# Dividing a prompt's attention probabilities on ACT in place of DVE

## The reference

```
h = rmsnorm(x);  [u | q | k | v | forget | gates] = h @ w_in        # width 4616
s = q k^T / 8 + c_q - c_k, masked (k_pos <= q_pos)
p = softmax(s);  att = p @ v                                        # fox_block
x = x + (sig(g0) * (pool @ w_up_pool) + sig(g1) * (att @ w_up_att)) @ w_out
x = x + hier_moe(rmsnorm(x))     # top-1 of 4 groups, top-2 of its 8 experts, 32 experts in all
y = rmsnorm_final(x)
```

## Time and profile before

| | |
|---|---|
| time, median of 3 runs | 720.68 us (717.95, 720.68, 722.97) |
| span of the profiled execution, first to last instruction | 716.0 us |
| its own time outside the span | not among the timed runs; the median is 4.7 us above the span, the fastest run 1.95 us |
| busy, share of span | PE 83%, PE weight load 51%, DVE 31%, ACT 12%, POOL 7% |
| instructions | 13798; DVE 549, ACT 232 |
| HBM traffic | 269 MB in all, mean 376 GB/s |
| instructions of the touched step | 4 reciprocals, 16 multiplications on DVE |

### The profile page before, as it was taken

How to read it: one execution, slowest core, us unless ns; L and a number is a source line. 1 busy time by engine, 2 the same in 40 slices (tenths; PEclk the granted TensorE clock), 3 DMA queues, 4 the chain that set the end, 5 groups by cost and what they waited for, 6 DMA issues and landing times.

```text
span 716.0 us, 13798 instructions
## 1 busy us (share of the span) xinstructions
PE 597.4 (83%) x6181; PEld 367.5 (51%) x6181; DVE 222.2 (31%) x549; ACT 88.5 (12%) x232; POOL 51.3 (7%) x57
## 2 busy tenths in 40 slices
PE   8999999999999999999677678675877767786683
PEld 7778777775573555555343344343443334443341
DVE  4259996972140362322111111111111111111113
ACT  2312232311101330000000000000000000000003
POOL 4136430112000000000000000000000000000000
PEclk9999999999999999999898878898788988899887
DMA  9985989987999399999999999999999999999981
GB/s 303 303 334 208 326 181 426 376 350 315 411 424 415 126 376 407 422 423 427 424 424 424 423 427 428 421 424 424 427 424 422 426 426 425 424 422 427 420 350 73
DMA packets 41379, 269.15 MB, mean 376 GB/s; under 512 B 9845, under 2 KB 10673, under 8 KB 22880
## 3 DMA queue, kind: packets, MB, share of 16 engines
q1 hardware_dynamic: 28960, 229.34, 79.2%
q0 software_dynamic: 3072, 35.19, 12.0%
q10 hardware_dynamic: 9287, 3.73, 2.1%
HBM read 266.01 MB, written 2.46 MB: 375 GB/s over the span
## 4 chain that ended last, share of the span: by engine, by line
DMA 49%; PE 38%; DVE 6%; issue 3%; ACT 2%; ACTq 1%; POOL 0%; SPq 0%; DVEq 0%; POOLq 0%
DMA ring<-w_up 43%; PE bank L1371 11%; PE bank L1613 4%; PE bank L1630 4%; PE bank L1476 3%; DMA ring<-w_in 3%; PE bank L1544 2%; DVE ring L1025 2%; PE bank L1387 2%; DMA ring<-cache_k,ridx 2%; PE bank L1355 2%; PE bank L1567 2%; PE bank L1402 1%; PE bank L1462 1%; DMA x<-x_prompt 1%
## 5 line engine op out<-in xcount | busy, mean ns | idle before, releaser
L1371 PE MATMUL bank<-ring,front 128*32 128x256 f32 x1856 | 160.9, 482 | 89.2 <-DMA ring<-w_up 78.1
L1371 PEld LDWEIGHTS bank<-ring,front 128*32 128x32 f32 x1856 | 86.1, 138 | 147.2 <-issue 123.4
L1233 DVE COPY front<-bank 128x256 f32<-128x256 f32 x32 | 13.6, 425 | 235.1 <-PE bank L1371 235.1
L1567 PE MATMUL bank<-hT,ring 128*128 128x264 f32 x256 | 59.8, 389 | 1.5 <-DMA ring<-w_in 1.1
L1387 PE MATMUL bank<-ring,front 128*32 128x256 f32 x928 | 55.4, 379 | 0.0
L848 ACT ACTIVATE front<-bank 128x128 f32<-128x128 f32 x32 | 8.9, 278 | 372.9 <-PE bank L1379 372.9
L1567 PEld LDWEIGHTS bank<-hT,ring 128*128 128x128 f32 x256 | 47.7, 190 | 11.2 <-issue 2.1
L1355 PE MATMUL bank<-front 128*32 128x256 f32 (+1 forms) x768 | 52.3, 385 | 0.3 <-DVE front L1136 0.3
L1476 PE MATMUL bank<-hT,ring 128*128 128x264 f32 x192 | 44.6, 389 | 0.0
L1243 DVE COPY front<-bank 128x256 f32<-128x256 f32 x32 | 13.6, 425 | 86.7 <-PE bank L1387 86.7
L1387 PEld LDWEIGHTS bank<-ring,front 128*32 128x32 f32 x928 | 30.0, 110 | 20.1 <-issue 0.5
(11 more groups left out here) (322 smaller groups left out, 565.7 us busy)
## 6 DMA issues: line engine op xcount, KB each, us to landing
ring<-w_gate SPq DMA_DIRECT2D x28, 2048.0 KB, 41.9
ring<-w_up SPq DMA_DIRECT2D x28, 2048.0 KB, 38.7
ring<-w_down SPq DMA_DIRECT2D x28, 2048.0 KB, 41.3
ring<-w_in SPq DMA_DIRECT2D x8, 2048.0 KB, 21.5
x<-w_gate SPq DMA_DIRECT2D x3, 2048.0 KB, 42.4
x<-w_up SPq DMA_DIRECT2D x3, 2048.0 KB, 38.0
x<-w_down SPq DMA_DIRECT2D x3, 2048.0 KB, 41.9
ring<-w_out SPq DMA_DIRECT2D x2, 2048.0 KB, 16.5
```

Of the source, the lines that this page charges most:

```text
L1371: last = m.matmul(bank[GATEUP][32 * g:32 * g + 32, 0:256], xgT[:, k % 2, k // 2], w[:, k, 256 * (g % 2):256 * (g % 2) + 256], start=k == 0 ...
L1567: last = m.matmul(out[:, 0:TOK], w[:, k, cols], hT[:, k, 0:TOK], start=k == 0, stop=k == DK - 1)
```

## The change

ACT gets a step `hnorm`. It waits for a new semaphore that DVE counts after the reciprocal, and does the four multiplications as copies with a scale from a column of `hinv`. DVE keeps the reciprocal alone and no longer waits for it. PE's wait for `s_probs` stays, with ACT counting it. The list of steps isn't changed.

```
+        s_hinv = sem("prompt_sums_inverted")
@@ ACT's stream
+                elif step == "hnorm":
+                    act.wait_ge(s_hinv, a + 1)
+                    for f in range(2):
+                        pr = probs[:, f]
+                        s.activation(pr[:, 0:P], pr[:, 0:P], ACT.Copy, scale=hinv[:, f, 0:1])
+                        s.activation(pr[:, P:3 * P], pr[:, P:3 * P], ACT.Copy, scale=hinv[:, f, 1:2]).then_inc(s_probs, 1)
                 elif step == "pT":
@@ DVE's stream
                     elif step == "hnorm":
                         dve.wait_ge(s_exp, 4 * a + 4)
-                        link(v.reciprocal(hinv, hsum))
-                        for f in range(2):
-                            pr = probs[:, f]
-                            v.tensor_scalar(pr[:, 0:P], pr[:, 0:P], hinv[:, f, 0:1], None, ALU.mult)
-                            v.tensor_scalar(pr[:, P:3 * P], pr[:, P:3 * P], hinv[:, f, 1:2], None, ALU.mult).then_inc(s_probs, 1)
+                        v.reciprocal(hinv, hsum).then_inc(s_hinv, 1)
```

## The result

The changed kernel takes 724.43 us (723.06 to 725.83, four runs) against 719.54 us for the kernel before in the same comparison: 4.9 us more, a ratio of 1.0070 with a 95% interval of 1.0041 to 1.0099. It is slower, clear of scatter, and within 1%. The profiled execution has a span of 722.8 us against 716.0.

The account below looks back on a forecast made before the run. PE's progress to SP's load at 248.81 us, then fixed loading, was taken as the bound. Stall 4.7 plus clock 1.9 less 0.86 gave 5.7 us over 720.7: 726.4 us, range 722 to 730.

Parts of the forecast that it names:

- the sum of 5.7 us: Whole kernel: 4.7 us of stall plus 1.9 of slower clock less 0.86 of saved wait, against the profiled execution.
- Pair 0 behind ACT's issues: At pair 0, ACT's copies wait behind its load issues; PE idles 4.1 us and `gate` 2 starts 4.7 us late.
- The copies: On ACT, four scaled copies per pair take 1.49 us, at least 1.1; the first f is ready after 0.79.
- The clock: After PE's pause at 94.3 us, a lower clock lengthens `gate` 2 by 1.9 us, bounds 0 and 2.9.
- The gain of 0.86 us: PE's wait for `m1` at 154.51 us goes away, which is all the change can gain.
- Pair 1 to 3 hidden: At pairs 1 to 3, the copies fit beside PE's gates and DVE has 4 us to spare: no further stall.
- the two waits of 1.7 and 2 us: DVE loses about 1.7 us at pair 2 and waits about 2 us at pair 3, behind late exponentials.
- The end moves one for one: Any delay of PE before SP's load at 248.81 us delays the kernel's end by the same amount.
- the one without a stall: Rival at pair 0: ACT's issues don't block the copies, only the 0.86 us is gained: 719.8 us, chance 0.12.
- the stall without the clock: Rival at pair 0: PE pauses but its clock stays up or drops under a microsecond: 724.5 us, chance 0.13.
- the table load: Rival at ACT's copies: table loads before and after, 8 x 1.28 us, mostly hidden: 728 us, chance 0.03.
- A second wait: Rival: PE also waits for a late `m1` or pair 3's copies, or a longer low clock: 728.5 to 731 us, chance 0.2.

Follow-up runs that it names:

- e1: The changed kernel, with ACT issuing the eight router loads after pair 0's division instead of ahead of it: 717.93 us, ratio 0.9993 to the kernel before.
- e2: The changed kernel, but DVE divides pair 0 as before and ACT only pairs 1 to 3: 718.81 us, ratio 0.9988 to the kernel before.
- e3: The kernel before, but pair 0 alone is divided on ACT: 723.29 us, ratio 1.0067.
- e5: The kernel before, no division moved, but PE waits at pair 0's transposes for a one-column ACT copy behind the router loads: 722.76 us, ratio 1.0047.
- e11: The changed kernel, with SP issuing the eight router loads instead of ACT: 717.74 us, ratio 0.9983 to the kernel before.
- e12: The kernel before, divisions on DVE, with SP issuing the eight router loads instead of ACT: 718.07 us, ratio 0.9990.
- e4: The changed kernel, with PE doing four idle products before its wait for pair 0's probabilities: 723.05 us, ratio 1.0056 to the kernel before.
- e9: The kernel of e1, with SP waiting for the router loads to land before it loads the weights of gates 8 to 11: 717.71 us, ratio 0.9977.
- e7: The changed kernel, with ACT issuing the router loads early, behind its evacuations of two projections of v: 728.92 us, ratio 1.0138 to the kernel before.
- e10: The changed kernel, with SP waiting for the router loads to land before it loads the weights of gates 8 to 11: 723.99 us, ratio 1.0071.
- e6: The changed kernel, with five of the eight router loads ahead of pair 0's division and three behind: 720.48 us, ratio 1.0016 to the kernel before.

## Why the prediction was right

The time lies in the range (722 to 730), the sign and the place were right, and the sum of 5.7 us compares with 4.9 in the times and 5.44 at SP's load. Point by point:

- *Pair 0 behind ACT's issues, 4.7 us.* Measured 4.66 in the trace; PE's wait 4.17 for 4.1 forecast. e1, e2, e3 and e5 show by themselves that it is this place, and that the division as such is not needed for the loss.
- *The copies, 1.49 us for four, first f after 0.79.* They ran from 97.75 to 99.24, 1.49 us. The Trainium skill ("ScalarE: Activation LUTs", what ACT_TABLE_LOAD costs) gives 280 ns and 0.833 ns a column for an instruction with a column as bias, of which 93 ns are for the column, whichever operand it is; an estimate from that for a column as scale is 387 and 493 ns. The rows agree (0.39 to 0.40, 0.49). The rule of the Trainium skill that the prediction named ("ScalarE: Activation LUTs", rules for kernel authors) holds for the durations, 0.35 us on DVE against 0.49 on ACT at 256 columns, but this cost lay off the path: e11 and e12 take the same 62.89 us.
- *The clock, 1.9 us.* Measured 1.68 in the changed kernel and 1.63 in e4 by taking it away. The bound of 2.9 was never near.
- *The gain of 0.86 us.* It is there: no wait at L1537. By the traces it is worth 1.02 us, so the parts are 4.66 + 1.68 - 1.02 = 5.32 us.
- *Pair 1 to 3 hidden.* Right in the sum, `m1` ending at 156.56 (156.2 forecast) and PE arriving at 160.04 (160.2). Wrong in the middle. I kept the page's arrival at 116.2 "for" DVE's timetable; it came at 118.7, by a trigger that I had not followed: DVE faster, slot free earlier, 2 MB load ahead of the small ones, POOL late. e9 shows the link. The loss that I placed at pair 2's exponentials therefore did not occur (DVE itself was later), and at pair 3 DVE waited 1.76 us one step earlier, for the transposes of pair 2 to free the buffer, not before the reciprocal. That `m1` ended within 0.4 us of the forecast is luck: a page 2.5 us late and this wait of 1.76 stood in for the two waits of 1.7 and 2 us that I had worked out.
- *The end moves one for one.* 5.44 us at SP's load, 4.9 in the medians; the profiled execution's span grew by 6.8, of which some 1.4 us appeared after 672 us, in PE's last wait for an expert's weights (L1371 at 666.48 and 681.26 before, L1374 at 671.83 and 688.12 changed). My ground for it was read too broadly: the earlier trace rows shows 421 GB/s for 300 to 320 us, and from 252 to 280 us the trace has less, 411 and then 380 GB/s, though at a share of 0.98. The median I started from, 720.68, was a little high, as the comparison's 719.54 shows; that and the 0.8 us of the sum are the 2 us between 726.4 and 724.4.

Of the rivals, the one without a stall is refuted by the 4.17 us, the stall without the clock by the 0.50, the table load by the trace of ACT, which has none at the copies. A second wait did occur, but in e1, where PE was early enough to meet its partners late.

## What to carry to other kernels

Before moving work to an idle engine, read what stands ahead of it in that engine's own order, load issues above all: an engine at 12% busy had no free moment in the 7 us that mattered. Then follow what the relieved engine does sooner, which slots it frees and which big transfers start ahead of small ones that somebody waits for. Small loads go best on a queue that nobody waits for, and a pause on PE costs its length and, when long, the clock behind it.

## What was unexpected in the hardware

- The time that an engine is held by issuing a small load varied widely. For 32 KB of the router's weights from ACT it was 0.61 to 1.70 us in the kernel before and 0.60 to 9.31 us in e7. For the 4 KB of `norm_ffn` it was 0.34 us from ACT at a DMA share of 1.01 (e7) and 8.68 us from SP at 1.03, behind two loads of 2 MB of the same queue (e11). The Trainium skill ("DMA: Bandwidth & Descriptors", issuing engines are not separate DMA queues) calls the time to issue usually small beside the DMA itself. Here landings of the router's weights took 2.5 to 4.0 us in the kernel before and 2.4 to 19.6 in e7, so the issues were a good part of them. What in the queue holds the engine, no run here shows.
- A small load was late behind a big one of another queue: 2 KB landed 3.1 us after its issue in the kernel before, and 8.5 and 9.2 us after it in the changed kernel and e1, where SP had issued a load of 2 MB 0.4 and 1.0 us ahead of it; 3.9 us with the big load held back (e9, e10).
- Pauses of PE of 1.44 and 2.36 us left the granted clock at 1.00 (e6, e5); those of 3.56, 3.88 and 4.17 us were followed by 0.50, the 1.2 GHz level, for about 3 us each (e3, e10, changed).
